# Moving the split weights' ring by 128 bytes in a two-block transformer kernel

## The chip, the cores and the metric

The kernel runs on one core of a Trainium2 chip. The metric is its device time in microseconds (us). A profile of one execution gives, for each engine, every instruction's start and length.

## What is computed

Two blocks, one after the other, on 256 tokens of width 1024, all in float32. The first block normalises and modulates tokens and context, projects both by w_in, runs a windowed attention and a bidirectional mLSTM, joins the two by w_out, and ends in a SwiGLU layer with hidden width 2816. The second block puts 16 meta tokens in front (272 tokens in all), runs a SwiGLU layer, a windowed attention and a gated linear attention joined by two gates, a projection, and another SwiGLU layer. Cut to the part that takes the time:

```
fx = swiglu(modulate(rms_norm(x, g_pre_ffn), sh_f, sc_f), w_ffn_in, w_ffn_out)          # 256 tokens
h  = h + 0.5 * swiglu_2(rmsnorm(h, ffn1_norm), ffn1_w_gate, ffn1_w_up, ffn1_w_down)     # 272 tokens
aq, ak, av, gq, gk, gv, gr, g_low, gate_a, gate_b = split(u @ w_in)                     # 272 or 256 tokens
h  = h + 0.5 * swiglu_2(rmsnorm(h, ffn2_norm), ffn2_w_gate, ffn2_w_up, ffn2_w_down)     # 256 tokens
```

## The kernel before

**Split products.** Each weight matrix is read once, in pieces of 1024 or 1408 columns per partition. SyncE's queue loads a piece into one of the four slots of the ring `raw` (L419). ScalarE copies it, rounded, to the same slot of `hi` (L621). VectorE subtracts: `lo` = `raw` - `hi` (L1143). Activations are split the same way into a high and a low part. Every product is then three matmuls: high weights by high activations, high weights by low activations, low weights by high activations (`split_mm`, lines L2005, L2006 and L2007; for some stages the same three are written out at L2134, L2203 to L2205 and around L2398). In nearly all stages the weights are the stationary operand (a tile of 128 x 128, 512 bytes per partition) and the activations the moving one. In the value and gate stages of the front (L2203 to L2205) it is the other way round: slots of `hi` and `lo` are the moving operand, 512 columns wide, and tiles of the normalised tokens are stationary.

**The order.** The order of the work is written out by hand for every engine. The stages on TensorE, with their moving operand:

- front, 0 to about 162 us: win0, winq (256 and 512 wide, moving n5H and n5L), winm, and winv and wino (512 wide, moving hi and lo), among small attention and mLSTM matmuls; w_ada's slabs are loaded and used in the same time
- wout (256 wide, mixH and mixL)
- gu0 (258 wide, n_high and n_low, a row of 1088 bytes), then dn0 (256 wide, g_high and g_low, a row of 1024 bytes)
- gu1 (272 wide, n_high and n_low, 1088 bytes), dn1 (272 wide, g_high and g_low, 1088 bytes)
- in2k (272 wide, n_high and n_low, a row of 1280 bytes), in2g and brb (256 wide; in2g reads n_high and n_low 16 columns in, rows of 1280 bytes), bra, wout2 (256 wide)
- gu2 (256 wide, mixH and mixL, rows of 1024 bytes), dn2 (256 wide, g_high and g_low, 1024 bytes)

"Row" is the stride from one k-tile of the moving operand to the next. gu stages have 11 steps of 96 products, dn stages 4 steps of 132. Before gu0 and gu1 the kernel issues some products of a slot with itself, only to keep TensorE working (`keep_clock`, L2484: stationary hi[:, 0, 0:128], moving hi[:, 0, 0:512]).

**Where tiles lie.** Tiles are placed one after the other in the order in which they are declared, in bytes per partition; a stack that is closed gives its place back. Behind `raw` (4 slots of 5632 bytes) come `slab_hi` (closed at once, so `hi` lies over it), `hi` and `lo` (22528 bytes each), `sinkn` (64), `negm` (128), then `stage` (closed, so `mixH` lies over it), `mixH` and `mixL` (8192 each), inv and rms (2048 each), three tables of 128 bytes, and then the tiles of the blocks. Counted from the start of `hi`:

| moving operand | bytes behind hi | modulo 256 |
|---|---|---|
| mixH | 45248 | 192 |
| n5H | 89216 | 128 |
| n_high | 66176 | 128 |
| n_high, 16 columns in | 66240 | 192 |
| g_high | 112320 | 192 |

`lo` lies 22528 bytes behind `hi`, and the low part of each moving operand a multiple of 256 behind its high part, so the three products of a split have the same distance modulo 256.

`negm` holds the negated maxima of the attention scores: VectorE writes a column (L1436, L1903), ScalarE reads it as a bias (L781, L797, L798). `sinkn` holds the negated sinks.

Of the kernel before, what the change touches and what calls it, by code (L numbers as in the profile page):

```python
# [14 lines left out]
P = 128  # L15
# [99 lines left out]
def program(nc, dr, out):  # L115
    with ExitStack() as root:
        def sbuf(stack, name, shape, dt=F32):
            return stack.enter_context(nc.sbuf_tensor(name, shape, dt))
# [12 lines left out]
        crow = sbuf(root, "crow", [P, D])  # L131
        R = sbuf(root, "R", [P, KD, TM])
        raw = sbuf(root, "raw", [P, RING, SLOT])
        slabs1 = ExitStack()
        slab_hi = sbuf(slabs1, "slab_hi", [P, RING, SLOT])
        slabs1.close()
        hi = sbuf(root, "hi", [P, RING, SLOT], F32R)
        lo = sbuf(root, "lo", [P, RING, SLOT], F32R)
        sinkn = sbuf(root, "sinkn", [P, 16])
        negm = sbuf(root, "negm", [P, 32])  # L140
        staged = ExitStack()
        stage = sbuf(staged, "stage", [P, 4, 1024])
        staged.close()
# [2655 lines left out]
```

## Time and profile before

| | |
|---|---|
| median of 3 runs | 968.3 us (967.9 to 972.03) |
| span of the profiled execution | 969.3 us |
| TensorE busy (matmuls) | 954.7 us |
| TensorE busy (weight loads) | 886.8 us |
| VectorE busy | 640.4 us |
| ScalarE busy | 494.7 us |
| GpSimd busy | 68.8 us |

The profile is of one execution, and its span runs from the first to the last instruction of the program. Matmuls are pipelined: the length of one is modelled and overlaps the next, so a count of matmuls in a window, or the start of one beside the start of another, says more than busy time. A few matmul records can be missing. Times in a trace are from the span's start.

### The profile page before, as it was taken

Reading aid. Unit: us, or ns where it says so; the run is one execution under the profiler, and the core shown is the slowest. Engines: PE = TensorE matmul, PEld = TensorE weight load, DVE = VectorE, ACT = ScalarE, POOL = GpSimd, SP = SyncE. Lnnn points to the kernel's source line nnn. Section 1 sums busy time; section 2 is a strip of 40 time slices with the busy share of each in tenths; the row PEclk is TensorE's granted clock in tenths of the full one; section 3 lists DMA queues with packets and bytes.
Section 4 is the critical chain, followed back from the end, with each engine's and each line's share of the span. In section 5 each row is a group of like instructions: output and inputs, shape, how many; then the busy total and the mean of one; then the engine's idle time right before and its main releaser. Section 6 shows DMA issues by size and latency. Waiting matters only on the chain.

```text
span 969.3 us, 19405 instructions
## 1 busy us (share of the span) xinstructions
PE 954.7 (98%) x7543; PEld 886.8 (91%) x7543; DVE 640.4 (66%) x990; ACT 494.7 (51%) x762; POOL 68.8 (7%) x100
## 2 busy tenths in 40 slices
PE   8999999999999999999999999999999999999997
PEld 3776778899999999899999999999989999999997
DVE  4788887687666774765555546665778666565654
ACT  3755547664454543554444434645565555444540
POOL 0012002200000021000000000200210100000000
PEclk9999999999999999999999999999999999999999
DMA  9982437546566795276665944663445567567841
GB/s 348 384 282 89 131 131 237 181 165 201 180 187 184 203 299 164 63 215 174 173 174 169 238 114 137 212 185 88 132 134 173 167 181 209 179 182 220 215 119 43
DMA packets 189184, 176.06 MB, mean 182 GB/s; under 512 B 7313, under 2 KB 177825, under 8 KB 188753
## 3 DMA queue, kind: packets, MB, share of 16 engines
q1 hardware_dynamic: 183456, 154.29, 53.7%
q0 software_dynamic: 4960, 17.64, 5.2%
q10 hardware_dynamic: 720, 3.49, 0.9%
q8 instruction: 31, 0.51, 0.2%
q14 instruction: 17, 0.13, 0.1%
HBM read 174.32 MB, written 1.05 MB: 181 GB/s over the span
## 4 chain that ended last, share of the span: by engine, by line
PE 88%; DVE 6%; DMA 2%; ACT 2%; issue 1%; SPq 1%; POOL 0%; DVEq 0%; ACTq 0%
PE acc L2005 24%; PE acc L2006 24%; PE acc L2007 24%; PE acc L2398 2%; DMA slab_hi<-in_w_ada 1%; DMA stage<-in_w_late 1%; PE acc L2203 1%; PE acc L2205 1%; PE acc L2204 1%; PE wk L2005 1%; DVE lo L1143 1%; PE wk L2007 1%; PE wk L2006 1%; PE wk L2702 1%; PE wk L2134 1%
## 5 line engine op out<-in xcount | busy, mean ns | idle before, releaser
L1143 DVE TENSOR_TENSOR lo<-raw,hi 128x1024 fp32r<-128x1024 f32 (+1 forms) x259 | 331.6, 1291 | 211.4 <-ACT hi L621 211.1
L621 ACT ACTIVATE hi<-raw 128x1024 fp32r<-128x1024 f32 (+1 forms) x260 | 283.6, 1099 | 133.7 <-PE acc L2007 123.5
L2005 PE MATMUL acc<-n_high,hi 128*128 128x272 f32 (+3 forms) x1016 | 290.8, 286 | 0.3 <-DVE hbuf L1671 0.3
L2006 PE MATMUL acc<-n_low,hi 128*128 128x272 f32 (+3 forms) x1016 | 289.4, 285 | 0.0
L2007 PE MATMUL acc<-n_high,lo 128*128 128x272 f32 (+3 forms) x1016 | 288.4, 284 | 0.0
L2005 PEld LDWEIGHTS acc<-n_high,hi 128*128 128x128 f32 (+1 forms) x1016 | 191.6, 189 | 2.7 <-issue 1.4
L2006 PEld LDWEIGHTS acc<-n_low,hi 128*128 128x128 f32 (+1 forms) x1016 | 191.1, 188 | 0.5
L2007 PEld LDWEIGHTS acc<-n_high,lo 128*128 128x128 f32 (+1 forms) x1016 | 191.0, 188 | 0.2
L2006 PE MATMUL acc<-g_low,hi 128*128 128x256 f32 (+1 forms) x528 | 149.1, 282 | 0.0
L2005 PE MATMUL acc<-g_high,hi 128*128 128x256 f32 (+1 forms) x528 | 148.9, 282 | 0.0
L2007 PE MATMUL acc<-g_high,lo 128*128 128x256 f32 (+1 forms) x528 | 148.7, 282 | 0.0
L2005 PE MATMUL acc<-mixH,hi 128*128 128x256 f32 x400 | 113.0, 282 | 0.5 <-DVE gab L1844 0.4
L2006 PE MATMUL acc<-mixL,hi 128*128 128x256 f32 x400 | 112.3, 281 | 0.0
L2007 PE MATMUL acc<-mixH,lo 128*128 128x256 f32 x400 | 112.3, 281 | 0.0
L2006 PEld LDWEIGHTS acc<-g_low,hi 128*128 128x128 f32 x528 | 99.8, 189 | 0.0
L2005 PEld LDWEIGHTS acc<-g_high,hi 128*128 128x128 f32 x528 | 99.2, 188 | 0.2 <-issue 0.2
L2007 PEld LDWEIGHTS acc<-g_high,lo 128*128 128x128 f32 x528 | 99.2, 188 | 0.0
L2006 PEld LDWEIGHTS acc<-mixL,hi 128*128 128x128 f32 x400 | 76.6, 192 | 0.0
L2005 PEld LDWEIGHTS acc<-mixH,hi 128*128 128x128 f32 x400 | 75.1, 188 | 1.4 <-DVE gab L1844 0.7
L2007 PEld LDWEIGHTS acc<-mixH,lo 128*128 128x128 f32 x400 | 75.1, 188 | 0.0
L566 POOL TENSOR_TENSOR sq<-sq 128x256 f32<-128x256 f32 (+1 forms) x28 | 25.6, 915 | 479.9 <-ACT sq L923 431.9
L923 ACT ACTIVATE sq<-R (+3 forms) x36 | 15.9, 440 | 57.6 <-DVE R L1715 49.9
(424 smaller groups left out, 1246.6 us busy)
## 6 DMA issues: line engine op xcount, KB each, us to landing
raw<-in_w_in SPq DMA_DIRECT2D x52, 512.0 KB, 4.1
raw<-in_w_ffn_in SPq DMA_DIRECT2D x44, 512.0 KB, 3.8
raw<-in_ffn_w_gate SPq DMA_DIRECT2D x44, 512.0 KB, 3.9
raw<-in_ffn_w_up SPq DMA_DIRECT2D x44, 512.0 KB, 3.8
raw<-in_ffn_w_down SPq DMA_DIRECT2D x32, 704.0 KB, 4.8
stage<-in_w_late POOLq DMA_DIRECT2D x24, 512.0 KB, 5.1
raw<-in_w_ffn_out SPq DMA_DIRECT2D x16, 704.0 KB, 6.2
raw<-in_w_out SPq DMA_DIRECT2D x16, 512.0 KB, 4.4
```

The costliest lines, as they stand in the source:

```text
L566: ins = pool.tensor_tensor(sq[:, 0, 0:width], sq[:, 0, 0:width], sq[:, k, 0:width], ALU.add)
L621: act.activation(hi[:, j, 0:width], raw[:, j, 0:width], ACT.Copy).then_inc(hi_ready, 1)
L923: act.activation(sq[:, k, 0:width], R[:, k, t0:t0 + width], ACT.Square).then_inc(sq_ready, 1)
L1143: dve.tensor_tensor(lo[:, j, 0:width], raw[:, j, 0:width], hi[:, j, 0:width].bitcast(F32), ALU.subtract).then_inc(lo_ready, 1)
L2005: pe.matmul(out_, wH, xH, start=start, stop=False)
L2006: pe.matmul(out_, wH, xL, start=False, stop=False)
L2007: return pe.matmul(out_, wL, xH, start=False, stop=stop)
L2134: ins = pe.matmul(bank[:, T * m:T * m + T], ws[:, j, w], xs[:, k, 0:T], start=k == 0 and m == 0 and n == 0, stop=k == KD - 1 and n == 2, s ...
L2203: pe.matmul(out_, n5H[:, k, rows], hi[:, k // 2, w], start=k == 0, stop=False)
L2204: pe.matmul(out_, n5H[:, k, rows], lo[:, k // 2, w], start=False, stop=False)
L2205: return pe.matmul(out_, n5L[:, k, rows], hi[:, k // 2, w], start=False, stop=k == KD - 1)
L2398: ins = pe.matmul(out_, ws[:, j, w], xs[:, k, :], start=k == 0 and m == 0 and n == 0, stop=k == KD - 1 and n == 2, skip_group_check=True)
```

## The change

One line is moved: `negm` is declared between `raw` and `slab_hi` instead of behind `sinkn`. So `negm` lies right behind `raw`; `slab_hi`, `hi`, `lo` and `sinkn` lie 128 bytes later. `raw` and all before it, and `mixH` and all behind it, keep their places. No instruction, wait or transfer is added, taken away or put elsewhere.

```
         raw = sbuf(root, "raw", [P, RING, SLOT])
+        negm = sbuf(root, "negm", [P, 32])
         slabs1 = ExitStack()
         slab_hi = sbuf(slabs1, "slab_hi", [P, RING, SLOT])
         slabs1.close()
         hi = sbuf(root, "hi", [P, RING, SLOT], F32R)
         lo = sbuf(root, "lo", [P, RING, SLOT], F32R)
         sinkn = sbuf(root, "sinkn", [P, 16])
-        negm = sbuf(root, "negm", [P, 32])
         staged = ExitStack()
```

## Rows read from the trace of the kernel before

**Rows 1.** Page, busy time by engine, and groups: busy us, mean ns | idle.

```profile
PE 954.7 (98%) x7543; PEld 886.8 (91%) x7543; DVE 640.4 (66%) x990; ACT 494.7 (51%) x762; POOL 68.8 (7%) x100
...
L1143 DVE TENSOR_TENSOR lo<-raw,hi 128x1024 fp32r<-128x1024 f32 (+1 forms) x259 | 331.6, 1291 | 211.4 <-ACT hi L621 211.1
L621 ACT ACTIVATE hi<-raw 128x1024 fp32r<-128x1024 f32 (+1 forms) x260 | 283.6, 1099 | 133.7 <-PE acc L2007 123.5
```

**Rows 2.** Busy time by stage: window, its us, engines' busy us (count), PEclk, DMA.

```profile
0.00:52.00 52.00, 47.41 (x249) 29.25 (x250) 31.04 (x72) 28.67 (x51) 4.72 (x15) 1.00 1.01 368
...
209.00:327.00 118.00, 118.00 (x977) 117.95 (x976) 80.73 (x114) 60.07 (x84) 0.00 (x0) 1.00 0.64 191
...
406.00:529.00 123.00, 122.69 (x979) 122.39 (x978) 71.79 (x73) 57.69 (x73) 0.00 (x0) 1.00 0.64 183
529.00:595.00 66.00, 66.00 (x527) 65.97 (x526) 35.93 (x40) 28.10 (x34) 4.66 (x6) 1.00 0.57 154
```

**Rows 3.** TensorE's waits: us in total, times, longest.

```profile
PE acc L2101 <- POOL cink L508: 2.5, 1, 2.5
```

**Rows 4.** TensorE alone in dn0, gu2 and dn2: busy us (count), PEclk, DMA.

```profile
327.40:386.90 59.50, 59.49 (x525) 1.00 0.77 222
782.00:897.00 115.00, 115.00 (x979) 1.00 0.67 194
898.00:959.50 61.50, 61.50 (x524) 1.00 0.48 129
```

**Rows 5.** Timeline of TensorE, first product after the sums and last of dn2.

```profile
781.53 0.47 PE L2005 MATMUL acc<-mixH,hi 128*128 128x256 f32 x1
...
959.77 0.28 PE L2007 MATMUL acc<-g_high,lo 128*128 128x256 f32 x1
959.90 0.16 PE L2738 MATMUL wk<-cst,sq 128*128 128x1 f32 x1
```

**Rows 6.** Timeline of TensorE, starts in two stretches of 24, and at 737.90.

```profile
671.42 0.28 PE L2007 MATMUL acc<-n_high,lo 128*128 128x256 f32 x1
...
672.48 0.28 PE L2007 MATMUL acc<-n_high,lo 128*128 128x256 f32 x1
...
676.73 0.28 PE L2005 MATMUL acc<-n_high,hi 128*128 128x256 f32 x1
...
677.41 0.28 PE L2005 MATMUL acc<-n_high,hi 128*128 128x256 f32 x1
...
737.90 0.36 PE L2005 MATMUL acc<-mixH,hi 128*128 128x256 f32 x1
```

**Rows 7.** Timeline of TensorE in the front and while it keeps the clock.

```profile
31.06 0.28 PE L2134 MATMUL wk<-n5H,hi 128*128 128x256 f32 x1
...
33.78 0.28 PE L2134 MATMUL wk<-n5H,lo 128*128 128x256 f32 x1
...
66.09 0.40 PE L2005 MATMUL wk<-n5H,hi 128*16 128x512 f32 x1
...
70.96 0.39 PE L2005 MATMUL acc<-n5H,hi 128*128 128x512 f32 x1
...
71.65 0.39 PE L2005 MATMUL acc<-n5H,hi 128*128 128x512 f32 x1
...
73.28 0.39 PE L2006 MATMUL acc<-n5L,hi 128*128 128x512 f32 x1
...
389.53 1.98 PE L2484 MATMUL acc<-hi 128*128 128x512 f32 x8
...
L2484 PE MATMUL acc<-hi 128*128 128x512 f32 x12 | 2.9, 390 | 0.0
```

**Rows 8.** TensorE by shape, 598.87 to 611.03 (L2006, L2007 alike); timeline in gu1.

```profile
L2005 PE MATMUL acc<-n_high,hi 128*128 128x272 f32 x32 | 9.3, 290 | 0.0
...
412.06 0.28 PE L2005 MATMUL acc<-n_high,hi 128*128 128x272 f32 x1
...
413.80 0.29 PE L2007 MATMUL acc<-n_high,lo 128*128 128x272 f32 x1
```

**Rows 9.** TensorE by shape, 70 to 160 us (L2204 and L2205 alike).

```profile
L2203 PE MATMUL acc<-hi,n5H 128*128 128x512 f32 x48 | 20.1, 419 | 0.0
```

**Rows 10.** Instructions of negm: ns least/median/most, first and last start.

```profile
L1436 DVE DVE_READ_ACCUMULATOR2_ANT negm<- x16: 82/83/89, 68.1 to 137.8; 128x1 f32 x16
```

More of the change, by code:

```diff
@@ L133, in program @@
         raw = sbuf(root, "raw", [P, RING, SLOT])
+        negm = sbuf(root, "negm", [P, 32])
         slabs1 = ExitStack()
@@ L139, in program @@
         sinkn = sbuf(root, "sinkn", [P, 16])
-        negm = sbuf(root, "negm", [P, 32])
         staged = ExitStack()
```

## The prediction

> **What bounds the kernel now.** I read the split of the execution by engine first, then the table by stage, then the waits, and last the matmuls one by one in order of time.
>
> TensorE is busy in 954.7 of 969.3 us [rows 1]. By stage, the long ones from 209 us on have it busy in practically every microsecond (118.00 of 118, 122.69 of 123, 66.00 of 66); the holes are in the first one, 47.41 of 52 us [rows 2]. Its waits are small: the longest is 2.5 us [rows 3]. VectorE and ScalarE are busy for 66% and 51% and wait for TensorE, not the other way round [rows 1]. The granted clock is 1.00 in each of these stages, the 2.4 GHz level [rows 2, 4]. So the time is the number of matmuls times the distance from one start to the next, and only something that changes that distance, or makes TensorE wait, can matter.
>
> Busy time says nothing of that distance, because matmuls overlap: a 512-wide one has a modelled length of 390 ns and the next starts after 227 to 233 ns [rows 7]. I take the distance from counts in windows and from start times. What I look for is whether products of the same size always come at the same distance. They don't.
>
> - First down stage (dn0): 525 products 256 wide in 59.5 us, 113.3 ns each. Last down stage (dn2): the same lines, the same operands, the same width, 524 in 61.5 us, 117.4 ns. The last gate-and-up stage (gu2) counts 979 in 115 us, 117.5 ns [rows 4]. I call these the fast step (113.3 ns) and the slow step; the windows cut a product at each end, and by start times the slow one is 117.8 ns (next point).
> - Which step a stretch takes is settled in its first few matmuls and then stays. Two stretches of 24 products with the same operands, 5 us apart, settle on different ones: 9 steps in 1.06 us from 671.42 to 672.48, 117.8 ns, but 6 steps in 0.68 us from 676.73 to 677.41, 113.3 ns [rows 6]. The stretch that starts at 737.90 is slow, and so is the one from 781.53 to 959.90, which no wait interrupts [rows 4 to 6].
> - Products 512 wide show the same thing. From the first window tile (n5) against a slot they start 0.228 to 0.241 us apart (1.63 us from 71.65 to 73.28 for 7 steps, 232.9 ns); the clock-keeping ones, a slot against itself, have 8 starts in 1.98 us with a modelled length of 0.39 us each, so (1.98 - 0.39)/7 = 227.1 ns [rows 7].
>
> **The change, part by part.**
>
> *Where things lie.* No instruction, wait, queue or DMA is added, removed or reordered. Three things move: the negated maxima (negm) to just behind raw; hi, lo and the early slab over hi by 128 bytes; sinkn by 128 bytes too. raw, mixH and everything behind keep their addresses. From the sizes in the code, hi and lo are 22528 bytes each per partition and the two small tables 64 and 128, so mixH stands 45056 + 192 = 45248 bytes after hi; every slot (5632 bytes) and every weight tile (512 bytes) is a multiple of 256. Counted modulo 256, the moving operand stands before the change 192 bytes after its weights in all 256-wide stages behind the front (mixH, g_high, the frames of n_high, and their low parts), and 128 after in the front (n5) and in in2k (n_high from its first column). After the change these become 64 and 0. The modulus is my choice: no row tells it. If what matters repeats every 128 bytes or less, the change does nothing, which is the second case below. That address has a part at all I read from two 272-wide stages at the same clock: in2k, where every row of the moving operand lies at the same place modulo 256, takes 126.7 ns (96 products in 12.16 us), and gu1, where the rows take turns, 124.3 ns (14 steps in 1.74 us from 412.06) [rows 8].
>
> *Stages that can't gain.* In gu0 (258 wide), gu1 and dn1 (272 wide) the moving row advances by 1088 bytes, 64 modulo 256. All four distances 0, 64, 128, 192 are taken in turn, before and after; the change only moves the turn by two rows. Their 307 us [rows 2] I cost at nothing.
>
> *Front and in2k, distance 128 to 0.* Distance 128 never shows the fast step: 256 wide it takes 2.72 us for the 23 steps from 31.06 to 33.78, 118.3 ns [rows 7]. Distance 0 stands in the trace once, 512 wide, at 227.1 ns. The front has 240 such products (48 on each of the three value-and-gate lines [rows 9], and by the code 32 on each of the three of the keys), 240 x (232.9 - 227.1) = 1.4 us, and by the code 144 products 256 wide from win0 and winq, 144 x (118.3 - 113.3) = 0.7 us. in2k has 192 products: at gu1's pace they would save 192 x (126.7 - 124.3) = 0.5 us. Between 0 and 2.6 us; I take 1.3, since the front is partly waiting.
>
> *256-wide stages, distance 192 to 64.* This is what counts, and no row has distance 64 alone. The bounds are the two nearest: the fast step, 113.3 ns, and distance 128's 118.3 ns. Fast today are dn0 (528), 144 in wout, 312 between 611 and 670 us and twelve of the sixteen stretches of 24 up to 737 us: 1272 products. Slow today are the other four stretches (96), then 360 products from 737.90 and 1512 from 781.53 to 959.90 (by the code 1056 - 72 + 528; 178.4 us, 118.0 ns each [rows 5]): 1968. If all settle on the fast step: 1968 x (117.8 - 113.3) = 8.9 us gained. If none does: 1272 x 5.0 + 1968 x 0.5 = 7.3 us lost.
>
> Which? Fast is what a stretch usually finds when it starts anew: of the sixteen stretches between 671 and 737 us twelve do. Distance by distance, 0 has the fast step, 192 (64 to one side) has both, 128 has none; 64 is 64 to the other side. If only the size of the distance matters, 64 behaves as 192 does: both steps exist, and every long stretch chooses anew. The one that holds 222 us today has the slow step, so it has more to gain than dn0's 60 us has to lose. The likeliest outcome is that it settles fast and that what is fast stays so: -8.9 - 1.3 = -10.2 us.
>
> *ScalarE and VectorE.* The split copies raw to hi (1099 ns mean) and subtracts (1291 ns) [rows 1]; raw and hi no longer lie at the same place modulo 256. VectorE waits 211 us for ScalarE's copies and ScalarE 123.5 us for TensorE [rows 1]: between 387 and 960 us neither sets a start, so 5% on either is covered. Uncovered is only the front, where they could move a microsecond. negm is written by an 83 ns instruction and read as a bias column [rows 10]; one column at another address costs nothing.
>
> A rule of the Trainium skill speaks against any effect. Its page "SBUF — State Buffer" (section "Who interferes with whom") gives TensorE two read ports, one for the moving operand and one for weights, and says that it never waits on anyone; "Operand start alignment" there knows only element size as a condition, and says that its runs timed nothing. By that rule the sum would be zero. The rows disagree at one point: the same width of 512 comes at 232.9 and at 227.1 ns with full-size weight loads in both. "TensorE: Matmul & The Clock Gate" ("Back-to-back issue gap") gives N/2.4 + 2.5 ns, 109.2 ns for 256 columns; neither step here reaches it.
>
> **The rivals.**
>
> *Nothing that counts changes (0.35).* The steps hang on the moving operand's address and on the moment of the start, and not on the weights'. For it: products with weight tiles of only 16 columns, whose addresses go on by 64 bytes from row to row, come at about the pace of whole tiles (4.87 us from 66.09 to 70.96 for 21 steps, 231.9 ns [rows 7]); so the size of the load hardly matters, and with it perhaps not its address. The long slow stretch stays slow, dn0 stays fast, and the front gives 0 to 2.6 us: 965.7 to 968.3 us. The two-port rule above is this rival.
>
> *Slower: distance 64 has no fast step (0.27).* Place: every 256-wide stage, dn0 first. Price: 7.3 us as above, less 0 to 2.6 us at the front: +4.7 to +7.3, 973.0 to 975.6 us. It decides as soon as over 1000 of the 1272 fast products fall to 118 ns. For it: fast steps are found in the trace at 192 and 0 only, and the slow step already lives at 192. Against it: gu1 takes distance 64 in turn with the others and is cheaper than in2k, which has 128 alone [rows 8].
>
> *Partly.* The long stretch is entered twice, at 737.90 and 781.53; if only the second turns fast, 1512 x 4.5 = 6.8 us, 960 to 961.5 us; it counts with the forecast.
>
> **How the numbers follow.** The sum is against the profiled execution, 969.3 us, 1.0 us above the median of 968.3; I take the difference from the median: 968.3 - 10.2 = 958.1 us. Chances: the forecast 0.38, with a range of its own of 957 to 962; nothing changes 0.35; slower 0.27. The range for 8 in 10 goes from 956.5, the forecast with the whole front (-8.9 - 2.6 = -11.5, 956.8) and a third of a microsecond more, to 975.5, the slower rival's upper end. A measurement of this kernel tells apart about 0.5%, 4.8 us: faster is under 963.5, slower over 973.1. Faster 0.38, same 0.35, slower 0.27.
>
> **What the profile would show.** Right: starts 0.113 us apart from 738 us on, and gu2 and dn2 shorter by 4%; gu0, gu1 and dn1 as long as before to 0.5 us; the 512-wide products at about 227 ns; in2k under 12.16 us for 96. Slower rival: dn0 over 62 us. Nothing-rival: each stage within 0.5 us of its row. Wrong altogether: a changed length of the rotating stages, or new waits of TensorE for the splits.

## The result, and the profile after

| | before | after |
|---|---|---|
| time, median (runs) | 970.87 us (20) | 972.93 us (20) |
| lowest to highest | 967.66 to 975.99 | 970.46 to 977.65 |
| span of the profiled execution | 969.3 | 971.4 |

The ratio after to before is 1.003, 95% interval 1.0016 to 1.0044: a hair slower, under the half per cent that I called no change. The forecast, 958.1 us, did not come. Over 20 runs each, before has a higher median than the three runs that I started from (968.3), and the time of such an execution is its span plus 1.8 us.

The page of after: engines, and the two groups of the splits.

```profile
PE 956.5 (98%) x7543; PEld 889.2 (92%) x7543; DVE 640.6 (66%) x990; ACT 494.6 (51%) x762; POOL 68.0 (7%) x100
...
L1143 DVE TENSOR_TENSOR lo<-raw,hi 128x1024 fp32r<-128x1024 f32 (+1 forms) x259 | 331.7, 1291 | 213.1 <-ACT hi L621 212.7
L621 ACT ACTIVATE hi<-raw 128x1024 fp32r<-128x1024 f32 (+1 forms) x260 | 283.4, 1098 | 134.6 <-PE acc L2007 124.1
```

Same work, same mean of a split: 1291 and 1098 ns, against 1291 and 1099 in [rows 1]. That raw and hi no longer lie at the same place modulo 256 bytes costs nothing. The 2 us must be in the distance between products, so I read counts by stage. After, busy time by stage (columns as in [rows 2]):

```profile
0.00:52.00 52.00, 47.10 (x249) 29.10 (x250) 31.01 (x71) 28.71 (x51) 4.74 (x15) 1.00 1.01 367
...
209.00:327.00 118.00, 118.00 (x976) 117.92 (x975) 80.53 (x114) 60.05 (x84) 0.00 (x0) 1.00 0.64 190
...
406.00:529.00 123.00, 122.69 (x978) 122.36 (x977) 71.64 (x73) 57.68 (x73) 0.00 (x0) 1.00 0.64 183
529.00:595.00 66.00, 66.00 (x526) 66.00 (x525) 36.18 (x40) 28.10 (x34) 4.65 (x6) 1.00 0.57 154
...
611.00:660.00 49.00, 49.00 (x448) 47.52 (x447) 31.04 (x41) 28.40 (x37) 3.15 (x2) 1.00 0.60 170
660.00:738.00 78.00, 77.53 (x664) 70.01 (x663) 53.52 (x126) 44.66 (x103) 9.62 (x6) 1.00 0.39 116
```

And of before, the two stages that [rows 2] leaves out:

```profile
611.00:660.00 49.00, 49.00 (x455) 47.55 (x454) 32.30 (x45) 28.84 (x37) 4.14 (x2) 1.00 0.60 174
660.00:738.00 78.00, 77.40 (x673) 69.46 (x672) 54.29 (x125) 45.91 (x104) 9.62 (x6) 1.00 0.40 120
```

The rotating stages keep their counts to one product (977, 979 and 527 in [rows 2]). Between 611 and 738 us the changed kernel gets through 7 and 9 products fewer in the same time: 16 products, 1.9 us. By start times, product for product, after is 0.2 us later when gu1 begins, 0.34 us at 611 us, 1.2 us at 660, 2.1 us at 738, and 2.1 us from there to the end. In before, 13 of the 17 stretches of 24 products between 671 and 739 us settle on 113.3 ns; in after 2 do, the others on 117.8 to 118.

The long stages, TensorE alone. A window also counts the products that reach over its ends, so the step is the window divided by the count less 2: 113.4 ns for 443 in 50 us, 117.6 for 427, and 117.6 for 852 in 100 us. dn0, gu2 and dn2 of after:

```profile
335.00:385.00 50.00, 50.00 (x443) 1.00 0.84 239
...
790.00:890.00 100.00, 100.00 (x852) 1.00 0.67 196
902.00:952.00 50.00, 50.00 (x427) 1.00 0.59 159
```

Before has 443, 852 and 426 in the same windows. So dn0 stays fast at distance 64, and the 222 us that were slow stay slow. What I meant to gain did not come, and the short stretches lost what they had.

In the front the 512-wide products got faster, as forecast for distance 0, but by half as much. The same lines, before and after, in the last group of twelve:

```profile
143.05 0.39 PE L2203 MATMUL acc<-hi,n5H 128*128 128x512 f32 x1
...
144.92 0.40 PE L2205 MATMUL acc<-hi,n5L 128*128 128x512 f32 x1
```

```profile
142.90 0.39 PE L2203 MATMUL acc<-hi,n5H 128*128 128x512 f32 x1
...
144.71 0.39 PE L2205 MATMUL acc<-hi,n5L 128*128 128x512 f32 x1
```

Eight steps in 1.87 us before, 233.8 ns; in 1.81 us after, 226 ns. That is the best case. These products come in short groups, most of twelve, that take several steps to settle: over all 203 steps inside the groups the mean goes from 232.3 to 229.2 ns. And the 256-wide ones of the front go from about 118.7 to about 120 ns. At 145 us after is ahead by only 0.2 us. in2k, by the same start times, has not changed: 13.40 us for its last 107 products, and a settled step of 126.7 ns, in both.

### The profile page after: what moved, and what is told of

Read it like the earlier page. It is cut to its first block, busy times and chain, and to the rows that moved or that the text cites. A ratio compares the mean times of both kernels' runs of the same rounds, so it can differ in the third digit from the quotient of the medians.

```text
span 971.4 us, 19405 instructions
## 1 busy us (share of the span) xinstructions
PE 956.5 (98%) x7543; PEld 889.2 (92%) x7543; DVE 640.6 (66%) x990; ACT 494.6 (51%) x762; POOL 68.0 (7%) x100
## 4 chain that ended last, share of the span: by engine, by line
PE 87%; DVE 7%; DMA 2%; ACT 2%; issue 1%; SPq 1%; POOL 0%; DVEq 0%; ACTq 0%
PE acc L2005 24%; PE acc L2006 24%; PE acc L2007 24%; PE acc L2398 2%; DMA slab_hi<-in_w_ada 1%; DMA stage<-in_w_late 1%; PE acc L2203 1%; PE acc L2204 1%; PE acc L2205 1%; PE wk L2005 1%; DVE lo L1143 1%; PE wk L2007 1%; PE wk L2006 1%; PE wk L2702 1%; PE wk L2134 1%
## 5 line engine op out<-in xcount | busy, mean ns | idle before, releaser
L1143 DVE TENSOR_TENSOR lo<-raw,hi 128x1024 fp32r<-128x1024 f32 (+1 forms) x259 | 331.7, 1291 | 213.1 <-ACT hi L621 212.7
L621 ACT ACTIVATE hi<-raw 128x1024 fp32r<-128x1024 f32 (+1 forms) x260 | 283.4, 1098 | 134.6 <-PE acc L2007 124.1
L2006 PE MATMUL acc<-n_low,hi 128*128 128x272 f32 (+3 forms) x1016 | 289.8, 285 | 0.0
L2007 PE MATMUL acc<-n_high,lo 128*128 128x272 f32 (+3 forms) x1016 | 288.7, 284 | 0.0
L2006 PEld LDWEIGHTS acc<-n_low,hi 128*128 128x128 f32 (+1 forms) x1016 | 191.0, 188 | 0.5
L2007 PEld LDWEIGHTS acc<-n_high,lo 128*128 128x128 f32 (+1 forms) x1016 | 190.9, 188 | 0.2
L2007 PE MATMUL acc<-g_high,lo 128*128 128x256 f32 (+1 forms) x528 | 148.7, 282 | 0.0
L2006 PE MATMUL acc<-g_low,hi 128*128 128x256 f32 (+1 forms) x528 | 148.6, 281 | 0.0
L2006 PE MATMUL acc<-mixL,hi 128*128 128x256 f32 x400 | 111.6, 279 | 0.0
L2007 PE MATMUL acc<-mixH,lo 128*128 128x256 f32 x400 | 111.6, 279 | 0.0
L2006 PEld LDWEIGHTS acc<-g_low,hi 128*128 128x128 f32 x528 | 99.2, 188 | 0.0
L2007 PEld LDWEIGHTS acc<-g_high,lo 128*128 128x128 f32 x528 | 99.1, 188 | 0.0
L2007 PEld LDWEIGHTS acc<-mixH,lo 128*128 128x128 f32 x400 | 75.2, 188 | 0.0
L2006 PEld LDWEIGHTS acc<-mixL,hi 128*128 128x128 f32 x400 | 74.9, 187 | 0.0
```

The costliest lines, as they stand in the source:

```text
L621: act.activation(hi[:, j, 0:width], raw[:, j, 0:width], ACT.Copy).then_inc(hi_ready, 1)
L1143: dve.tensor_tensor(lo[:, j, 0:width], raw[:, j, 0:width], hi[:, j, 0:width].bitcast(F32), ALU.subtract).then_inc(lo_ready, 1)
L2006: pe.matmul(out_, wH, xL, start=False, stop=False)
L2007: return pe.matmul(out_, wL, xH, start=False, stop=stop)
```

## The experiments

Two theories. **Distance**: what counts is how far the moving operand stands from its weights, modulo 256 bytes, and where a distance has two steps, the moment at which a stretch is entered chooses. **Moment only**: addresses do not matter; the change shifts entries, and entries choose. The change cannot tell them apart, because it moves both. Six kernels with an m in front are products alone: they leave out the whole computation and write zeros, so only the distance between their products is read. Step means the distance from start to start once a stretch has settled. In the timeline a stretch is one line; its length, less 0.28 us for the last product and 0.20 us for the first step, divided by the products less 2, is the step.

**The pace at each distance (m1).** 16 distances, four entries each, 36 products from `hi` against `mov[:, d // 4 + ...]`.

> This kernel leaves the whole computation out: it only issues products 256 columns wide, a weight tile of 128 x 128 in hi by a tile in mov, in the reduced-precision float32 type of the kernel, and writes zeros. For each of 16 distances from the weights to the moving operand, 0 to 480 bytes in steps of 32, it issues four runs of 36 products, each run behind two plain matmuls of another width (128, 130, 132, 134), so that the runs start at different moments. Theory A (the distance modulo 256 decides which steps exist, and the moment of the start chooses): steps of 113.3 and 117.8 ns at 0, 64 and 192, none of 113.3 at 128 (118.3), the table for 256 to 480 the same as for 0 to 224; at 64 fewer runs at 113.3 than at 192. Rival B (the weights' address does not matter, only the moment of the start): every distance shows the same mix of the two steps. Rival C (the modulus is 512 or 128): the table repeats after 128 bytes, or not at all.

Distances 0, 32, 64, 128 and then the first two entries of 192:

```profile
29.60 4.55 PE L167 MATMUL acc<-mov,hi 128*128 128x256 f32 x36
...
48.65 4.46 PE L167 MATMUL acc<-mov,hi 128*128 128x256 f32 x36
...
67.27 4.49 PE L167 MATMUL acc<-mov,hi 128*128 128x256 f32 x36
...
105.07 4.52 PE L167 MATMUL acc<-mov,hi 128*128 128x256 f32 x36
...
142.85 4.34 PE L167 MATMUL acc<-mov,hi 128*128 128x256 f32 x36
147.40 4.48 PE L167 MATMUL acc<-mov,hi 128*128 128x256 f32 x36
```

By start times: 120.0, 116.7, 117.8, 118.8, and 113.3 or 117.8 at 192 (three entries of four fast). 96 has 120.0, 160 118.8, 224 118.3; 256 to 480 repeat these eight. The modulus of 256, which I had only assumed, is right, and "moment only" falls: at most distances all entries agree. Here the moving operand moves and the weights stay; in the next two kernels it is the other way round.

**The ring at the two other distances (e1, e2).**

```diff
         raw = sbuf(root, "raw", [P, RING, SLOT])
+        sinkn = sbuf(root, "sinkn", [P, 16])
+        negm = sbuf(root, "negm", [P, 32])
...
-        sinkn = sbuf(root, "sinkn", [P, 16])
-        negm = sbuf(root, "negm", [P, 32])
```

e1 puts both tables ahead (256-wide stages at 0, front and in2k at 192); e2 only sinkn (128 and 64).

> Both small tables (sinkn and negm) stand in front of hi: the ring lies 192 bytes later than before, all behind it as before. The 256-wide stages behind the front then have distance 0, the front and in2k 192. Theory A: distance 0 finds the step of 113.3 ns most easily (the clock-keeping products show it at 0), so gu2 and dn2 turn fast: about 222 us at 117.8 become 213.5, some 8 us less than before, 959 to 963 us in the median beside 970.9. Rival B: within 2 us of before. Rival D (fast steps at all distances are chance): anything from 8 us less to 7 us more, differing stage by stage with no order.

> Only sinkn (64 bytes) stands in front of hi: the ring lies 64 bytes later. The 256-wide stages behind the front have distance 128, the front and in2k 64. Theory A: no stage has 113.3 ns; dn0 goes from 60.0 to 62.6 us, wout and the stretches from 611 to 737 us lose too, and 1272 fast products at 5 ns each give 6 us more than before; the long slow stretch gains or loses under 1 us: 976 to 978 us. Rival B: within 2 us of before.

e1 took 981.34 us, ratio 1.0096 (1.0081 to 1.0111); e2 980.01, 1.0085 (1.0071 to 1.0099). dn0 and gu2, first of e1, then of e2:

```profile
335.00:385.00 50.00, 50.00 (x419) 1.00 0.85 238
...
790.00:890.00 100.00, 100.00 (x836) 1.00 0.64 184
```

```profile
335.00:385.00 50.00, 50.00 (x424) 1.00 0.84 237
...
790.00:890.00 100.00, 100.00 (x845) 1.00 0.65 185
```

50/417 = 119.9 ns at distance 0 and 50/422 = 118.5 at 128, as m1 gives them, in the 256-wide stages behind the front, with no fast stretch (a few of e2's take up to 120.1 ns). My expectation for e1 was wrong by 20 us, and by the same inference as the prediction: I took the fast step of 512-wide products at distance 0 for a property of the distance, and it does not carry over to another width. e2 came out somewhat above its 976 to 978.

**The change with all distances put back (e3).**

```diff
+        negm = sbuf(root, "negm", [P, 32])
...
         sinkn = sbuf(root, "sinkn", [P, 16])
-        negm = sbuf(root, "negm", [P, 32])
+        sbuf(root, "pad_r", [P, 32])
```

> The change, and with it everything behind lo moved by 128 bytes as well (a pad behind sinkn), so that every distance from weights to moving operand is that of before, and only raw stands 128 bytes nearer to neither. Theory A: the stages are those of before (dn0 60.0 us, the stretches from 611 to 737 us fast again), median within 1 us of before. If the absolute address of the weights, or the distance from raw to hi in the splits, costs the 2 us of the change, it is 2 us over before as the change is.

966.76 us, ratio 0.9943 (0.9922 to 0.9964), its highest run (970.16) under the lowest of before in that comparison (970.51). The stretches up to 738 us are fast again, which clears the change: the loss came from the distance, not from moving negm. That e3 beats before was not expected. Its distances are the same, but in its trace two long stretches happened to be fast: 738 to 771 us, and dn2:

```profile
902.00:952.00 50.00, 50.00 (x443) 1.00 0.60 159
```

dn2 did not begin fast in e3. It came out of gu2 at 117.8 ns, and changed behind one long step after its 34th product, which before has too (before, then e3):

```profile
901.50 0.37 PE L2005 MATMUL acc<-g_high,hi 128*128 128x256 f32 x1
901.71 0.28 PE L2006 MATMUL acc<-g_low,hi 128*128 128x256 f32 x1
```

```profile
901.58 0.37 PE L2006 MATMUL acc<-g_high,hi 128*128 128x256 f32 x1
901.78 0.28 PE L2007 MATMUL acc<-g_low,hi 128*128 128x256 f32 x1
```

To the nanosecond the step is 210 in before, and 117.8 follows; it is 205 in e3, and 113.3 follows. So the stretch that the prediction calls uninterrupted up to 959.90 us is entered anew at 901.5.

**Finer distances (m2).** Steps of 8 bytes, eight entries each.

> Leaves the whole computation out and writes zeros: products 256 wide alone, 30 at a stretch, at distances 32 to 96 and 160 to 256 bytes in steps of 8, each entered eight times at slightly different moments (entry products 128 to 135 wide). Distance alone: each distance has one step whatever the moment, the fast 113.3 ns appears at 192 in about six entries of eight and nowhere else among the coarse ones (64: 117.7, 0: 120.0). Distance with moment: 64 too shows 113.3 ns in at least one entry of eight, as the first down stage of the changed kernel did, and 192 shows both steps. What I look for besides: whether a distance beside 192 (184, 200) has the fast step in all eight, or whether the fast step belongs to multiples of 64 alone; I expect 184 and 200 between 113.3 and 118.5.

Two entries at 64, one at 184, two at 192:

```profile
176.86 3.78 PE L167 MATMUL acc<-mov,hi 128*128 128x256 f32 x30
180.85 3.65 PE L167 MATMUL acc<-mov,hi 128*128 128x256 f32 x30
...
418.65 3.85 PE L167 MATMUL acc<-mov,hi 128*128 128x256 f32 x30
...
447.00 3.66 PE L167 MATMUL acc<-mov,hi 128*128 128x256 f32 x30
450.86 3.78 PE L167 MATMUL acc<-mov,hi 128*128 128x256 f32 x30
```

113.3 ns appears at 64 in one entry of eight and at 192 in three, and at none of the other twenty distances (116.6 to 121.6). With the eight entries of m1 and the two of m3 at each of these distances, that is one entry of 18 at 64 and ten of 18 at 192. Two steps are not peculiar to these two: 32 has 116.7 or 117.8, and 80 has 118.3 or 120.0. Beside 192 there is no gain but a loss: 184 and 200 take 120.0 and 120.2 (I had expected 113.3 to 118.5).

**Widths and weight tiles (m3).**

> Leaves the whole computation out and writes zeros: products alone, at distances 0 to 224 bytes in steps of 32, two entries each, for moving tiles 256 wide with weight tiles of 128, 64 and 16 columns, and 258, 272 and 512 wide with 128 columns, and 512 wide with 16. If the load of the weights collides with the reading of the moving tile, the spread over distances (6.7 ns at 256 wide and 128 columns) shrinks with the columns: under 4 ns at 64 and under 1 ns at 16. If only the addresses of starts count, 16 columns show the same eight numbers as 128. 512 wide with 128 columns: 227 at distance 0 and 231 to 233 at 128, as the front before and after. 272 wide: 123 to 127 with a spread of the same 3 to 7 ns; averaged over 0, 64, 128 and 192 it gives the rotating stages' 125.1.

| distance | 256 wide, 128 columns | 64 columns | 16 columns | 272 wide, 128 | 512 wide, 128 |
|---|---|---|---|---|---|
| 0 | 120.0 | 113.3 | 113.4 | 125.3 | 226.7 |
| 32 | 116.6 | 118.9 | 116.6, 120.0 | 126.0, 125.5 | 233.3 |
| 64 | 117.8 | 116.6 | 113.4 | 126.7 | 228.8 |
| 96 | 120.0 | 116.6 | 116.6 | 126.7, 125.6 | 233.3 |
| 128 | 118.8 | 116.7 | 120.0, 113.3 | 126.7 | 232.7 |
| 160 | 118.8 | 117.2, 120.0 | 116.6 | 123.3 | 234.2 |
| 192 | 113.4, 117.8 | 119.1 | 113.3, 120.0 | 123.3 | 233.3 |
| 224 | 118.4 | 116.7 | 113.4 | 125.3, 126.7 | 233.3 |

(Two numbers where the two entries differ.) Two kinds are not in the table: 258 wide takes 119.2 to 122.2 ns, and 512 wide with 16 columns 230.0 to 231.7. At distance 0 the loads of 128, 64 and 16 columns, and the 512-wide products at 0 and 128:

```profile
29.81 3.83 PE L167 MATMUL acc<-mov,hi 128*128 128x256 f32 x30
...
93.72 3.66 PE L167 MATMUL acc<-mov,hi 128*64 128x256 f32 x30
...
157.08 3.67 PE L167 MATMUL acc<-mov,hi 128*16 128x256 f32 x30
...
352.10 7.09 PE L167 MATMUL acc<-mov,hi 128*128 128x512 f32 x30
...
411.08 7.22 PE L167 MATMUL acc<-mov,hi 128*128 128x512 f32 x30
```

At 256 wide both expectations for the loads fail. The spread over distances does not shrink with a smaller load (6.7 ns at 128 columns, 6.7 at 16), and the eight numbers are not the same either: the size of the load shifts which distances have the fast step. At 512 wide it does shrink, from 7.5 ns with 128 columns to 1.7 with 16, which no account here explains. So the load takes part, but not simply as traffic. At 512 wide with 128 columns, 0 and 128 differ as they do in the real front. The mean of 0, 64, 128 and 192 at 272 wide, 125.5, lies between the 124.9 ns of gu1 and the 125.9 of dn1. in2k fits at two distances of three: 126.7 ns before (128) and 123.3 in e1 (192), but it keeps 126.7 after (0), where products alone take 125.3.

**Can the entry be made fast? (m4, m5, m6)** One small plain product between stretches of 24: at distance 192 (m4), at 64, 128 and 0 (m5), and in the real order of high and low parts (m6).

> Leaves the whole computation out and writes zeros: distance 192 alone, thirteen kinds of a single product put between stretches of 24, for two entries. If the two steps are stable rhythms between which only the moment of a start chooses, most nudges leave a stretch in the rhythm that it had or change it at once, and none gives a step other than 113.3 or 117.8; a nudge that takes slow to fast and leaves fast alone would be the means to make the real kernel's last 222 us fast (8 us). If the step drifts with something else (heat, clock, position in the program), the same nudge gives different outcomes in its four repetitions.

> Leaves the whole computation out and writes zeros: as the kernel of nudges, but at the changed kernel's distance 64, with single plain float32 products 16 to 152 columns wide (in steps of 8) between stretches of 24, and five widths each at distances 128 and 0. If 64 has two steps as 192 has, with other odds: some widths settle on 113.3 ns, fewer than at 192 (one entry in eight did at 64 and three in eight at 192); I expect 2 to 6 of the 18 widths. If 64 has in truth only the slow step, none. At 128 and 0 nothing fast either way: 118.8 and 120.0.

> Leaves the whole computation out and writes zeros: products 256 wide in the real kernel's order of three (high weights against high, high against low, low against high) with all four tiles at the same place modulo 256, stretches of 24, at distances 64 and 192, entered twice each, with one small plain product of 16 to 152 columns behind every stretch. If the real order is what keeps 64 slow: 64 shows 117.8 ns in nearly all of its 72 stretches and 192 shows 113.3 ns in most. If only the moment differs between the changed kernel and the products alone: 64 shows 113.3 ns as often as 192 does, and what differs is the first step behind the small product (199 to 201 ns where fast followed, 203 ns where slow did).

m4, two stretches with a 16-column product between:

```profile
31.93 3.07 PE L167 MATMUL acc<-mov,hi 128*128 128x256 f32 x24
34.84 0.29 PE L182 MATMUL wk<-plain 128*128 128x16 f32 x2
34.98 2.99 PE L167 MATMUL acc<-mov,hi 128*128 128x256 f32 x24
```

The first is slow, (3.07 - 0.48)/22 = 117.7 ns; the second, behind the small product, settles on 113.3. In m4 every stretch behind a product of 32 to 130 columns ended on 113.3 ns, for both entries; behind 132 columns it was slow, behind 134 fast again. Such a product costs 0.24 us (2.955 us from one to the next, less 24 x 113.3 ns). At 128 and 0 nothing came under 118 and 120.0 ns. But at 64 fourteen of eighteen widths were fast throughout, where I expected 2 to 6, and in the real order of products 59 of 72 stretches at 64 and 60 of 72 at 192. So 64 does have the fast step, and products alone keep it there as often as at 192. These counts are not so many draws, though: fast and slow come in unbroken rows (at 64 in m6, 29 and then 30 fast ones), because nearly every stretch follows a fast one in the same way. A single small product of 16 or 24 columns straight behind a slow stretch stood four times at each distance in m4 to m6, and turned two of the four at both; with 32 columns and more that was not tried with products alone.

**One entry turned in the real kernel (e7).**

```diff
+            set_free(0, USE["dn2"])
+            pe.matmul(acc[:, 0, 0:32], ones, ones[:, 0:32], start=True, stop=True)
             down("dn2", 2, T)
```

> The kernel before with one such product alone, ahead of dn2. Moment: gu2 stays at 117.8 ns and dn2's 528 products turn to 113.3, 2.4 us less 0.24: ratio 0.9977, dn2 61.5 to 62.2 us before and 59.9 to 60.2 here. Otherwise dn2 stays as it was and the kernel takes 0.24 us more.

968.79 us, ratio 0.9983 (0.9967 to 0.9999). The small product, the first three products of dn2, and dn2's window:

```profile
896.97 0.30 PE L2736 MATMUL acc<-cst 128*128 128x32 f32 x2
897.11 0.36 PE L2005 MATMUL acc<-g_high,hi 128*128 128x256 f32 x1
897.31 0.28 PE L2006 MATMUL acc<-g_low,hi 128*128 128x256 f32 x1
897.43 0.28 PE L2007 MATMUL acc<-g_high,lo 128*128 128x256 f32 x1
```

```profile
790.00:890.00 100.00, 100.00 (x851) 1.00 0.68 199
902.00:952.00 50.00, 50.00 (x444) 1.00 0.59 159
```

gu2 as before, dn2 from 426 to 444: as expected for "moment at distance 192". (The long step after dn2's 34th product is gone too, and the products from 754 us to about 774 happen to be fast in this trace, with nothing changed ahead of them.)

**Five and two entries turned, at 192 and at 64 (e5, e6, e9, e8).** e5 is before and e6 the change with five such products (at 738 us, at both first groups of gu2, behind its sum of squares, ahead of dn2); e9 is before and e8 is e3 with only the last two.

> The kernel before with five small plain float32 products of 32 columns (ones by ones, into a bank that the next product overwrites): ahead of the stretch at 738 us, at gu2's two first groups, at the first group behind gu2's sum of squares, and ahead of dn2. Each costs 0.12 us by the kernel of nudges (24 products and one nudge took 2.955 us against 24 times 113.3 ns, less the pause: 0.24 us). If the long slow stretch is slow only because of the moment at which it is entered: 1968 less 96 products turn from 117.8 to 113.3 ns, 8.4 us, less 1.2 us for the nudges: ratio 0.9925, 963 to 965 us where before gives 971, with 113.3 ns from 738 us to the end. If the moment is not the cause: before plus 1.2 us, 972.

> The changed kernel with the same five small products, at distance 64. If 64 has the fast step with worse odds: at most one of the four stretches turns (0 to 2.5 us gained, 1.2 lost), 971 to 974 us, and 117.8 ns for most products from 738 us on. If 64 behaves as 192 once the entry is right (what my prediction rested on): 965 us, as the kernel before with the same products.

> The kernel before with the same two small plain products. gu2's 960 and dn2's 528 products turn from 117.8 to 113.3 ns, 6.7 us, less 0.5 us: ratio 0.9936, 965 us where before gives 971. If gu2 turned in the kernel with five small products only by a combination with the earlier ones: dn2's 2.4 us alone, 969 us.

> The changed kernel with everything behind the small tables 128 bytes later too (all distances as before), and two small plain products: at the first group behind gu2's first chunk, and ahead of dn2. If the moment of entry decides at distance 192: gu2 960 products at 113.3 ns and dn2 too, 4.3 + 0 to 2.4 us less than the same layout without them, which took 966.8; less 0.5 us for the products: 961 to 963 us, ratio 0.990 to 0.992. If e3's gain was an accident of its job: 965, as the next kernel.

| | distance | small products | median | ratio to before | interval |
|---|---|---|---|---|---|
| e5 | 192 | 5 | 967.81 | 0.9961 | 0.9944 to 0.9978 |
| e6 | 64 | 5 | 975.47 | 1.0049 | 1.0031 to 1.0068 |
| e9 | 192 | 2 | 966.23 | 0.9931 | 0.9910 to 0.9952 |
| e8 | 192 | 2 | 965.69 | 0.9933 | 0.9910 to 0.9956 |

(e9 and e8 stand beside a before of 972.78, e5 and e6 beside one of 971.18.) dn0, gu2 and dn2 of e9, then gu2 and dn2 of e6:

```profile
335.00:385.00 50.00, 50.00 (x427) 1.00 0.86 239
...
790.00:890.00 100.00, 100.00 (x885) 1.00 0.71 203
902.00:952.00 50.00, 50.00 (x444) 1.00 0.58 155
```

```profile
790.00:890.00 100.00, 100.00 (x852) 1.00 0.67 195
902.00:952.00 50.00, 50.00 (x427) 1.00 0.59 159
```

e9 does 885 products where before does 852: 100/883 = 113.3 ns. The gain of e9 is what was expected. e8 was to take 961 to 963 us if the gain of e3 belonged to its layout, and 965 if that gain was an accident: it took 965.69, as e9 did, and in its trace gu2 was fast already ahead of the small product. So e3's 0.6% is not shown to come from its layout. e5's ratio fell 3.5 us short. In its trace it takes 215.8 us from the first product at 738 us to the last of dn2, before 221.9 (737.90 to 959.77): 6.1 gained of 7.2. The first of its five products came behind 24 that were fast already, and the stretch from 754 us was slow all the same (144 products to 771 us, 146 in before). The rest of the shortfall is open. In the four traces with small products at 192 they met a slow stretch four times (e5 twice, e7, e9) and turned it each time. The same products at distance 64 turned nothing. e9 also shows the lottery: this time dn0, at the same distance, with the same code ahead of it as in before, went slow, 427 for 443, 2.2 us. Such draws would explain why one kernel's runs spread over 968 to 976 us; as only one execution of each kernel has a trace, this is not shown.

**Other entries at 64 (e10, e11).** e6 with the small products' moving operand shifted.

> The changed kernel with the same five small products, their moving operand taken 64, 128, 192, 64 and 128 bytes further on (in their order in the program), which changes what the load of the next weights meets. If the moment of entry is all: at least one of the five stretches settles on 113.3 ns at distance 64, with a first step of 201 ns or less in place of 203. If distance 64 is slow in the kernel for another reason: all five at 117.8 ns, 975 us as the kernel with unshifted ones.

> The same with shifts of 32, 96, 160, 192 and 32 bytes. As the run before it: at least one of five stretches fast if the moment decides, none and 975 us if not.

976.11 and 974.84 us, one run each, beside 970.76: none of the five stretches fast in either. The first step behind the small product stayed at 203 ns in both, so the shift did not move the entry and the test did not reach its question. Start times of e6, whose gu2 is slow:

```profile
787.16 0.30 PE L2019 MATMUL acc<-cst 128*128 128x32 f32 x2
787.30 0.37 PE L2005 MATMUL acc<-mixH,hi 128*128 128x256 f32 x1
787.50 0.28 PE L2006 MATMUL acc<-mixL,hi 128*128 128x256 f32 x1
```

Read to the nanosecond: at 64, products alone mostly enter behind the small product with first steps of 200 or 201 and then 113 ns and are fast at once; the kernel enters with 203 and 121 and is slow. At 192 the kernel enters behind it with 199 to 203 ns and ends fast each time, after two to five steps on the way. The kernel's other stretches say the same. A stretch here is 18 products or more, 256 wide, behind the front, without a pause past its first step. Over the six traces at 192 (before, e3, e5, e7, e8, e9) 162 of 201 settle fast; over the two at 64 (after, e6), 9 of 67. Sorted by the first step:

| first step | fast at 192 | fast at 64 |
|---|---|---|
| 199 to 207 ns | 64 of 64 | 0 of 23 |
| 225 to 228 ns | 0 of 24 | 0 of 17 |

So the moment of entry picks the step, and the same moment picks another one at 64 than at 192. This is how many of the short stretches between 611 and 738 us lost their fast step; others were entered later than in before (three between 683 and 715 us with a first step of 226 ns for 221 or 222). A first step of 200 ns or so is not enough by itself, since in m2 it was followed by either step at 192. That 64's fast rhythm is entered from fewer moments fits all of this. Once, in e6, a stretch at 64 also fell from 113 to 118 ns on its way, behind 17 steps and without a pause (at about 741.9 us). Why the kernel enters 2 ns later than the products alone is open, and so is what sets the 5 ns between the long steps of e3 and before.

## Why the prediction was wrong

- *What bounds the kernel, and that only the step of the products can matter*: held. Nothing else changed in after.
- *Rotating stages, splits, negm, at nothing*: held (counts within one product, 1291 and 1098 ns). Of the stretches between 671 and 738 us I had left one out: 13 of 17 were fast, not twelve of sixteen.
- *Modulus 256, and that the address has a part*: held, now shown by m1, e1 and e2 instead of assumed, and e3 shows that it is the distance. The two-port rule of the Trainium skill ("SBUF — State Buffer", section "Who interferes with whom": TensorE never waits on anyone) gives no term for this; 113.3 to 120.0 ns by distance, at the same clock and load, disagrees with it if it is read to cover TensorE's own two operands.
- *Front and in2k, -1.3 us*: mis-sized. The 512-wide products gained 3.1 ns each over their short groups, not 5.8, so about 0.7 us of the 1.4. I gave the 144 products of 256 the fast step of 512-wide ones at distance 0; m1 and e1 have 120.0 ns there, so they lost. in2k gained nothing. Net 0.2 us at 145 us; the 0.3 us that this sum leaves over is open.
- *"If only the size of the distance matters, 64 behaves as 192 does"*: the step that failed. Both steps do exist at 64 (dn0 at 113.4 ns in after; m2, m5, m6), but the odds are others: 2 of 17 short stretches where 192 had 13. I reasoned from two distances to a third by symmetry, and m1 has none: 96 and 160 take 120.0 and 118.8, 32 and 224 take 116.7 and 118.3.
- *"Fast is what a stretch usually finds when it starts anew", so the 222 us would turn*: failed apart from the distance. Entries are not draws with fixed odds. Before and after enter at 781 us through the same six plain products, and gu2 is slow in every trace at 192 or 64 without a small product of its own: before, after, e3, e7. Nor is it one stretch: dn2 is entered anew at 901.5 us.
- *The slower rival*: its mechanism is the one that came, with the wrong extent. It wanted over 1000 of the 1272 fast products slow. dn0's 528 stayed fast; most of the other 744 went slow, and with entries that were not settled anyway that gave 0.4 us in wout and 1.8 us between 611 and 738, not 4.7. The gain at the front took 0.2 us back.
- *The base*: I put the profiled execution 1.0 us above the median. With 20 runs its 971.1 us (span plus 1.8) is nearly the median itself, and single runs differ by 8 us. My range, 956.5 to 975.5, holds the result only because it was wide.

## What to carry to other kernels

When TensorE is the bound, count starts by stage and compare stages that have the same width: two paces for the same product (here 113.3 and 117.8 ns) mean that something other than the work sets it. The place of the moving operand after its weights, modulo 256 bytes, is worth 1% of this kernel between its best and worst value, and is best measured with products alone for each width and weight tile, since none of it could be inferred from a neighbour. Where two paces exist, a small product ahead of a long stretch can pick the faster one (0.7% at distance 192, e9; nothing at 64, e6); check with several runs, because each long stretch draws anew.

## What the hardware showed that was not expected

- The distance modulo 256 sets the step of 256-wide products from 113.3 to 121.6 ns, in no simple order, and a change of 8 bytes at 192 costs 6.7 ns (184: 120.0).
- At 64 and at 192 the same two steps exist, each stable for hundreds of products; at 192 a plain product of 32 columns turned the slow one into the fast one for 0.24 us, four times of four.
- The best distance depends on width and weight columns: 192 for 256 wide with 128 columns, 0 with 64 columns, 160 or 192 for 272 wide (123.3), 0 for 512 wide (226.7).
- The changed kernel's twin with every distance restored (e3) ran 0.6% faster than before; with the two small products (e8) it was no faster than before with them (e9).
- The first step of a stretch tells its pace: in the kernel at 192, 199 to 207 ns was followed by 113.3 in 64 cases of 64, and 225 to 227 ns by 117.8 in 24 of 24.
